# Where the second half's operands get their low parts in a Strassen-form MLP: four kept in DRAM, and the sums and low parts of a weight group on one engine

## The reference, cut to what matters

```python
hn = rmsnorm(h, norm2_g[l])
ff = jnp.square(jax.nn.relu(jnp.einsum('bsd,df->bsf', hn, w_mlp_in[l])))
h = h + jnp.einsum('bsf,fd->bsd', ff, w_mlp_out[l])
```

## Time and profile before

| | before |
|---|---|
| median of three runs | 2073.66 us (2071.78 to 2073.93) |
| the profiled execution's own time | 2072.65 us |
| its span, first to last instruction | 2070.9 us |
| PE busy | 2033.8 us (98%) |
| DVE / ACT / POOL busy | 1374.6 / 932.5 / 756.7 us |
| mean granted TensorE clock | 0.995 of full |

### The profile page before, as it was taken

The page is one execution under the profiler, slowest core; times in us unless marked ns, Lnnn a source line. Parts: engine busy times, 40 slices in busy tenths (PEclk is TensorE's granted clock), DMA queues, the critical chain, the costliest instruction groups (busy, mean ns, idle before and its releaser), DMA issues. The chain is left out here.

```text
span 2070.9 us, 26149 instructions
## 1 busy us (share of the span) xinstructions
PE 2033.8 (98%) x9474; PEld 1678.6 (81%) x9474; DVE 1374.6 (66%) x1925; ACT 932.5 (45%) x1325; POOL 756.7 (37%) x786
## 2 busy tenths in 40 slices
PE   8999999999999999999998899999999999999998
PEld 7787888888888878888886688888788888888887
DVE  3899968787778972765568655556665546555475
ACT  4456663364244561455555444544333323333253
POOL 5544465234225442644446444444120202202031
PEclk9999999999999999999999899999999999999999
DMA  6884457455555545444442233333968566565675
GB/s 219 282 276 153 143 204 274 163 167 188 194 195 193 181 165 198 143 138 144 141 142 98 87 122 128 122 132 143 365 220 303 183 225 234 189 225 179 209 238 180
DMA packets 173537, 387.32 MB, mean 187 GB/s; under 512 B 15232, under 2 KB 64480, under 8 KB 173408
## 3 DMA queue, kind: packets, MB, share of 16 engines
q1 hardware_dynamic: 153536, 313.28, 44.6%
q10 hardware_dynamic: 19872, 72.36, 10.0%
HBM read 297.51 MB, written 88.08 MB: 186 GB/s over the span
## 5 line engine op out<-in xcount | busy, mean ns | idle before, releaser
L1938 DVE TENSOR_TENSOR down_lo<-down_raw,down_hi 128x1536 fp32r<-128x1536 f32 x112 | 201.6, 1800 | 232.1 <-ACT down_hi L1452 232.1
L82 PE MATMUL acc<-down_hi 128*128 128x512 f32 x896 | 348.5, 389 | 0.0
L83 PE MATMUL acc<-down_lo,down_hi 128*128 128x512 f32 x896 | 348.5, 389 | 0.0
L84 PE MATMUL acc<-down_hi,down_lo 128*128 128x512 f32 x896 | 348.5, 389 | 0.0
L1452 ACT ACTIVATE down_hi<-down_raw 128x1536 fp32r<-128x1536 f32 x112 | 166.8, 1489 | 359.5 <-PE acc L84 193.6
L1729 DVE SCALAR_TENSOR_TENSOR acc<-u_sb,cw_col,acc 128x512 f32<-128x512 f32 x464 | 313.3, 750 | 0.3
L1379 ACT ACTIVATE ring_hi<-ring_sum 128x512 fp32r<-128x512 f32 x145 | 91.6, 632 | 272.3 <-DVE ring_sum L1840 272.3
L82 PE MATMUL acc<-xT_hi,wt 128*128 128x512 f32 x512 | 204.6, 400 | 0.2 <-DVE u_sb L2012 0.2
L84 PE MATMUL acc<-xT_hi,wt 128*128 128x512 f32 x512 | 199.8, 390 | 0.0
L83 PE MATMUL acc<-xT_lo,wt 128*128 128x512 f32 x512 | 199.4, 389 | 0.0
L82 PEld LDWEIGHTS acc<-down_hi 128*128 128x128 f32 x896 | 168.2, 188 | 35.0
(11 more groups left out here) (290 smaller groups left out, 4460.1 us busy)
## 6 DMA issues: line engine op xcount, KB each, us to landing
wt<-w_kept SPq DMA_DIRECT2D x168, 512.0 KB, 3.3
down_raw<-f_kept ACTq DMA_DIRECT2D x109, 512.0 KB, 4.2
raw_w<-in_w_mlp_in SPq DMA_DIRECT2D x32, 1024.0 KB, 5.5
f_kept<-f_tile SPq DMA_DIRECT2D x128, 256.0 KB, 2.0
down_raw<-in_w_mlp_out SPq DMA_DIRECT2D x64, 512.0 KB, 3.7
w_kept<-wt SPq DMA_DIRECT2D x48, 512.0 KB, 5.3
down_raw<-in_w_mlp_out SPq DMA_DIRECT2D x64, 256.0 KB, 3.0
down_more<-f_kept ACTq DMA_DIRECT2D x29, 512.0 KB, 5.2
```

The lines of the kernel that those rows point to most:

```text
L82: nc.tensor.matmul(out, w_hi, x_hi, start=first, stop=False, skip_group_check=onto)
L83: nc.tensor.matmul(out, w_hi, x_lo, start=False, stop=False, skip_group_check=onto)
L84: return nc.tensor.matmul(out, w_lo, x_hi, start=False, stop=last, skip_group_check=onto)
L1938: nc.vector.tensor_tensor(down_lo[slot][:, :], down_raw[d % DOWN_RAW][:, 512:], down_hi[slot][:, :].bitcast(F32), ALU.subtract).then_inc(d ...
```

## The change

It touches the 29 Strassen groups and nothing in the mixer or in the down projection's own loop.

- **Four low parts kept.** In groups 8 to 10, ACT makes the high part of half an operand at a time in a spare tile (`pre_split`), DVE its low part in another (`pre_low`), and SP stores it in DRAM (`pre_stores`, eight stores of 512 KB). These are Strassen's operands 2, 5, 3 and 7 of the second half. At the turn ACT starts their load into place (four of 1 MB) and makes the high parts again.
- **Sums.** The sum for operand 1 (h11 + h22) is made ahead in group 11, in the two spare places. The sums for 6 and 4, and the low parts of 1, 6 and 4, stay at the turn, all on DVE and in halves of 1024 columns.
- **POOL's work moved.** `a_low` of all seven places and the three `f_sum` of a group are on DVE. POOL keeps two instructions of one column in each of groups 0 to 7.
- **Order.** DVE's slot is now: add the weights of product k + 4 (`UP_LEAD = 4`), combine product k, low part of product k + 4, one `f_sum` in slots 0 to 2, then the turn's work. The row tiles are loaded, normalised and transposed one group earlier.

```diff
+UP_LEAD = 4
+        spare_hi = over("g_row", "spare_hi", [P, 2, 512], F32R)
+        spare_lo = over("y_sb", "spare_lo", [P, 2, 512], F32R, 4 * KB)
+        mul_kept = nc.dram_tensor("mul_kept", [len(PRE_LOW), P, 4, 512], F32).ap()
...
 w1_free(w):
-                    sp.wait_ge(a_lo_g, upto(NQ * s + 1, LO_ON_POOL))
-                    sp.wait_ge(a_lo_v, upto(NQ * s + 4, LO_ON_DVE))
+                    sp.wait_ge(a_lo, NQ * s + max(UP_SINGLE) + 1)
...
 SP up_group(s):
                 for p in (3, 7, 1, 6):
                     f_store(w - 1, p)
-                    if p == 7 and 1 <= s <= HT:
-                        nat_load(s - 1)
+                    if p == 7 and s < HT:
+                        nat_load(s)
+                pre_stores(s, range(0, 3))
...
+                pre_stores(s, range(3, NQ))
...
 POOL up_group(s):
-                w = group(s)
-                a_low(NQ * s + 3)
-                late_sums(w - 1)
...
+                if s < HT:
+                    nat_rstd(s)
...
 ACT:
+            def pre_split(i):
+                m, part = PRE_LOW[i // 2], i % 2
+                act.wait_ge(hn_ok, HT)
+                act.wait_ge(tr_ok, 2 * HT)
+                if m in (3, 7):
+                    act.wait_ge(pre_ok, (1 if m == 3 else 3) + part)
+                wait(act, pre_lo, i)
+                nc.scalar.activation(spare_hi[:, :, :], mul_again_src[m][:, 2 * part:2 * part + 2, :], ACT.Copy).then_inc(pre_hi, 1)
+            def mul_again(m):
+                act.wait_ge(prod_pe, used(m))
+                if m in PRE_LOW:
+                    i = PRE_LOW.index(m)
+                    act.wait_ge(pre_st, 16 * (2 * i + 2))
+                    act.dma_start(mul_lo[m].bitcast(F32), mul_kept[i]).then_inc(mul_ld[m], 16)
+                    nc.scalar.activation(mul_hi[m], mul_again_src[m][:, :, :], ACT.Copy).then_inc(mul_hi_ok, 1)
...
 DVE:
+            def pre_low(i):
+                m, part = PRE_LOW[i // 2], i % 2
+                dve.wait_ge(pre_hi, i + 1)
+                if i == 0:
+                    dve.wait_ge(tr_pe, 2 * HT)
+                else:
+                    dve.wait_ge(pre_st, 16 * i)
+                nc.vector.tensor_tensor(spare_lo[:, :, :], mul_again_src[m][:, 2 * part:2 * part + 2, :],
+                                        spare_hi[:, :, :].bitcast(F32), ALU.subtract).then_inc(pre_lo, 1)
...
                 for s in range(NS):
                     for k in range(NQ):
+                        j = NQ * s + k + UP_LEAD
+                        if j < NQ * NS:
+                            a_add(j)
                         if k > 0:
                             combine(s, k)
-                        j = NQ * s + k + LEAD
-                        if LEAD < j < NQ * NS:
-                            a_add(j)
-                            turn(s, k)
+                        if j < NQ * NS:
                             a_low(j)
+                        if k in F_SUM_AT:
+                            f_sum(group(s) - 1, F_SUMS[F_SUM_AT.index(k)])
+                        turn(s, k)
...
             def down_pass():
                 d_low(2)
+                for p in F_SUMS:
+                    f_sum(NW - 1, p)
                 d_add_parts(LEAD)
...
 PE product(s, q):
-                pe.wait_ge(*((a_lo_g, upto(j, LO_ON_POOL)) if q in LO_ON_POOL else (a_lo_v, upto(j, LO_ON_DVE))))
+                pe.wait_ge(a_lo, j + 1)
...
+                elif s == TURN and m in PRE_LOW:
+                    pe.wait_ge(mul_hi_ok, hi_again(m))
+                    pe.wait_ge(mul_ld[m], 16)
...
+PRE_LO_AT = ((8, 4), (8, 6), (9, 1), (9, 3), (9, 6), (10, 1), (10, 4), (10, 6))
+PRE_SUM_AT = ((9, 4), (9, 5), (10, 2), (10, 3), (11, 1), (11, 3))
```

More of the change, by code:

```diff
@@ L472, in hybrid_block @@
         f_sum_ok = sem("f_sum_ok")
-        f_st = {p: sem(f"f_st{p}") for p in range(1, NQ + 1)}
+        f_st = {p: sem(f"f_st{p}") for p in (1, 3, 4, 6, 7)}
         a_sum = sem("a_sum")
         a_hi = sem("a_hi")
-        a_lo_v = sem("a_lo_v")
-        a_lo_g = sem("a_lo_g")
+        a_lo = sem("a_lo")
         prod_pe = sem("prod_pe")
@@ L484, in hybrid_block @@
         pre_ok = sem("pre_ok")
+        pre_hi = sem("pre_hi")
+        pre_lo = sem("pre_lo")
+        pre_st = sem("pre_st")
+        mul_ld = {m: sem(f"mul_ld{m}") for m in PRE_LOW}
         mul_hi_ok = sem("mul_hi_ok")
@@ L815, in nat_load, with pre_stores @@
                 sp.dma_start(nat[:, :], h_t[:, HT + t, :]).then_inc(hn_ld, 16)
+            def pre_stores(s, slots):
+                for i, at in enumerate(PRE_LO_AT):
+                    if at[0] == s and at[1] in slots:
+                        m, part = divmod(i, 2)
+                        sp.wait_ge(pre_lo, i + 1)
+                        sp.dma_start(mul_kept[m, :, 2 * part:2 * part + 2, :], spare_lo[:, :, :].bitcast(F32)).then_inc(pre_st, 16)
             def up_group(s):
@@ L1801, in add_again @@
+            def add_again(m):
+                dve.wait_ge(prod_pe, used(m))
+                src, op = (h12, ALU.add) if m == 6 else (h21, ALU.subtract)
+                for part in range(2):
+                    c = slice(2 * part, 2 * part + 2)
+                    ins = nc.vector.tensor_tensor(mul_sum[m][:, c, :], src[:, c, :], sum1_again[part][:, :, :], op)
                 ins.then_inc(mul_sum_ok, 1)
-            def pre_sum(tile, op):
-                dve.wait_ge(tr_ok, 2 * HT)
-                nc.vector.tensor_tensor(tile[:, :, :], tile[:, :, :], h22[:, :, :], op).then_inc(pre_ok, 1)
@@ new lines, in turn, with f_sum @@
+                if (s, k) in PRE_SUM_AT:
+                    pre_sum(PRE_SUM_AT.index((s, k)))
+                for m in MUL_SUM_AGAIN:
+                    if (s - TURN, k) == ADD_AGAIN_AT[m]:
+                        add_again(m)
+                for m in LOW_AGAIN_AT:
+                    if (s - TURN, k) == LOW_AGAIN_AT[m]:
+                        low_again(m)
+            def f_sum(w, p):
+                a, b, op, out = {7: (F21, F22, ALU.subtract, f_tile[:, F21, :]), 1: (F11, F22, ALU.add, f_sum1[:, :]),
+                                 6: (F12, F11, ALU.subtract, f_tile[:, F12, :])}[p]
+                dve.wait_ge(f_ok[a], w + 1)
+                dve.wait_ge(f_ok[b], w + 1)
+                if p == 1:
+                    dve.wait_ge(f_st[1], w * 16)
+                elif p == 7 and w == N_PLAIN - 1:
+                    dve.wait_ge(f_sum_ok, w * len(F_SUMS))
+                nc.vector.tensor_tensor(out, f_tile[:, a, :], f_tile[:, b, :], op).then_inc(f_sum_ok, 1)
@@ L1918, in up_pass @@
                             mul_low(7, mul_sum[7], 5)
-                        if k == 6 and 1 <= s <= HT:
-                            nat_normalise(s - 1)
+                        if k == 6 and s < HT:
+                            nat_normalise(s)
             def d_add_parts(d):
@@ L2293, in up_pass @@
                     for q in range(NQ):
-                        if q == 2 and 2 <= s <= HT + 1:
-                            nat_transpose(s - 2)
+                        if q == 2 and 1 <= s <= HT:
+                            nat_transpose(s - 1)
                         product(s, q)
@@ L2629 @@
 F_SUMS = (7, 1, 6)
+F_SUM_AT = (0, 1, 2)
 TR_BANKS = [(0, 1), (4, 5)]
```

158 lines of the change are left out of this document (66 added, 92 removed).

## The result

The change takes 2049.19 us (median of four runs, 2048.61 to 2050.61) where the kernel before takes 2073.20 in the runs beside it (2071.78 to 2073.93). The ratio is 0.9886, with a 95% interval of 0.9869 to 0.9903. So it is faster by 24.0 us, and the forecast of 2052 was 2.8 us too high. The profiled execution of the changed kernel took 2049.39 us, with a span of 2047.4.

A forecast was written before the change was run, and what follows sets the result against it. PE was busy 98% of the span, its main loss being the turn, where DVE stood behind POOL's wide instructions. 27.3 us won less 1.9, 3.2 and 0.6 is 21.6; 2073.7 less that gives 2052 us, range 2046.5 to 2060.

The forecast's parts named there:

- What is taken away: The turn's 24.3 us and two waits for POOL in the first and last group, about 1.5 each: 27.3 us gone.
- Steady load at nothing: Plain groups: DVE's work of 13.6 us in a group of 19.0 costs PE nothing.
- the seam: Passage to the down projection: three f_sum ahead of the fourth step's weights cost nothing, with 2 us as bound.
- Groups 8 to 11: DVE full in groups 9 and 10, waits 1.8 us for a store at 9.3; PE loses 1.9 us at 11.0 and 11.1.
- two restarts: Slow first matmul after a PE wait: about 0.1 us for each of six waits, 0.6 in all.
- the rival of slow stores: Stores of kept parts take 5 us and DVE waits at each: 8 in place of 1.9, so 2058; chance 0.13.
- The turn: Slots 12.3 to 13.0: DVE's queue makes PE lose 0.7 at 13.2, 0.4 at 13.3, 1.5 at 13.4, 0.6 at 14.0: 3.2 us.
- the first rival: DVE copes wholly, with shorter chains than the timetable and no PE wait: 2046; chance 0.1.
- no lower clock: No clock drop taken at the turn; a rival had twice 3.2 us there and a lower-clock stretch, 2058; chance 0.12.
- The slower rival: DVE becomes the bound in every group, with a mean slot of 2.9 us: 2089; chance 0.04.

The follow-up runs named there:

- the dummies: Changed kernel plus idle POOL instructions of 1024 columns in groups 14 to 25: reading tiles once a group 2049.33 us, seven times 2145.9; only writing, seven times, 2049.15.

## Why the prediction was right

**What is taken away: 27.3 us, right.** The turn's standing still, its lower clock and the two waits for POOL in the first and last group are all gone, and no wait for POOL is left. But the reason given was only a part of it. Moving POOL's wide instructions to DVE and nothing else gives 7.4 us. All of the change but the kept parts gives 15.4 to 15.8, and the kept parts the last 8. The sum came out right because I had taken away the whole of the turn and then costed what DVE's new queue would make anew (3.2 us); the experiment without kept parts shows that this second step, not the first, carries the kept parts' value.

**Steady load at nothing: right.** I counted 13.6 us of DVE's work in a plain group of 19.0. A plain group of the changed kernel has 13.8:

```profile
1170.00:1189.00 19.00, 19.00 (x86) 15.73 (x85) 13.80 (x21) 9.81 (x16) 0.00 (x0) 1.00 0.36 125
```

No PE wait stands in the plain groups after the turn up to the end, nor at the seam, where the low part of step 3 is in time with the three f_sum ahead of it. With a lead of three the plain groups have no wait either; what the longer lead covers is in groups 10 and 13, where 2.6 us come back without it.

**Groups 8 to 11: 1.9 us and two restarts (2.1), measured 1.5.** The mechanism is as forecast: DVE waits at slot 9.3 for the store of 9.1, and PE at 11.0 and 11.1. The sizes were off, and one figure of the working does not fit the rest: a store that starts "some 3 us" before DVE comes to 9.3 and lands in 3.3 leaves a wait of 0.3, not 1.8. The 1.8 needs a lead of 1.5 us, and that is what the trace has: the store starts at 1059.60, right behind the start of the f_sum's store, and DVE is free at 1061.20. DVE's wait, and the transfers from 860 to 1440 us, the answer to the earlier trace rows:

```profile
1062.55 1.22 DVE L1819 TENSOR_TENSOR spare_lo<-h,spare_hi 128x1024 fp32r<-128x1024 f32 x1 [1.35 <-DMA mul_kept<-spare_lo]
```

```profile
nat<-h_dram SPq DMA_DIRECT2D x8, 512.0 KB, 3.4
mul_kept<-spare_lo SPq DMA_DIRECT2D x8, 512.0 KB, 2.9
hT_lo<-mul_kept ACTq DMA_DIRECT2D x2, 1024.0 KB, 5.3
```

The store lands in 2.9 us, not 3.3, and the wait is 1.35 instead of 1.8. The straight line between the store of 256 KB and the load of 1 MB (3.1), from which I had gone up, was nearer. The page of before also had 48 stores of 512 KB from another stage, with a median of 5.3 us (`w_kept<-wt`, at 33 to 342 us), which spoke for the rival of slow stores and which I had not weighed. The fit in the Trainium skill, "DMA: Bandwidth & Descriptors", section "Anatomy of one DMA", is given there for transfers that GpSimd starts; used as an estimate for this store, which SP starts, it makes 3.2 us, 0.3 above the measured 2.9. The late starts at 11.0 and 11.1 are 0.97 and 0.49 us, where I had 1.4 and 0.5.

**The turn: 3.2 us and four restarts (3.6), measured 2.4.** By the distance between starts, 13.2 lost 0.1 us (forecast 0.7 and a restart), 13.3 lost 0.3 (0.4), 13.4 lost 1.5 (1.5), its slow start another 0.1 and 14.0 lost 0.4 (0.6). The term that was too large is DVE's start. I let it enter slot 12.3 at 0.9 us after the start of 12.4, because ACT would hold up slots 1 and 2. It entered at 0.27 (1116.46, with 12.4 at 1116.19), and its slots ended at 4.5, 8.0, 12.3 and 16.5 us instead of 5.2, 8.7, 13.0 and 17.2: all by the same 0.6 to 0.7. Where I had counted too much is not shown for certain, since the working gives the 0.9 as one figure. ACT's timeline has a likely place, the start of a transfer:

```profile
1111.81 0.33 ACTq L1366 DMA_DIRECT2D mul_lo<-mul_kept  x1
1111.88 0.61 ACT L1389 ACTIVATE ring_hi<-ring_sum 128x512 fp32r<-128x512 f32 x1
1112.46 1.92 ACT L1367 ACTIVATE mul_hi<-h 128x2048 fp32r<-128x2048 f32 x1
```

The start of the transfer lies beside the activation before it, so ACT loses less than the 0.34 us that I counted for each start; in slots 12.1 and 12.2 DVE waits 0.21 us for ACT in all. The loads landed in 5.3 to 6.9 us, up to 0.6 more than I had allowed, and PE waited for none. And what DVE comes to late is what I said, the low part of operand 4:

```profile
1134.66 2.35 DVE L1828 TENSOR_TENSOR xT_lo<-mul_sum,xT_hi 128x1024 fp32r<-128x1024 f32 x2
```

It ends at 1137.01, and product 13.4 starts at 1137.12.

**Sum.** Forecast 27.3 less 5.7, measured 27.3 less 3.9. From one profiled execution to the other, 2072.65 less 2049.39 are 23.3, where I had 21.6: that is 1.7 of the 2.8 us. The rest is the step to the median. I carried over that the median stands 1.0 above the profiled execution of before; of the changed kernel it stands 0.2 below. Both errors lie on the same side, so the total did not come out by one cancelling the other. (The range's lower end, 2046.5, leaves out the first rival's 2046, which the text says it takes in.)

**The rivals.** DVE did not cope wholly. The stores are fast. There is no lower clock: the longest wait is 1.19 us and the clock reads 1.00 behind it. The slower rival is excluded by 691 ns for the weights' sum: the 874 of the earlier trace rows were POOL's doing, which the dummies show from the other side. Its first half, the advice to hand work from a full VectorE to another engine (the Trainium skill, "Perfetto Trace Analysis", section "Optimizing Scalar/DVE Operations"), would have cost 7 us here with GpSimd as that engine, by the run with the three sums given back. Its own warning about the shared read port is what decides. What I had wrong in my own weighing was the size of the small instructions. The prediction charged POOL's wide ones with the turn and its small ones with two waits of 1.5 us. They also cost 6 to 7 us where DVE is full. The earlier trace rows showed them, as 874 ns where 690 are due, but no wait of PE in before did, since its groups 9 and 10 were not full.

What stays open: low parts given back to POOL without the sums were not run, so the 7 us of the sums and the 8 of both do not say what the low parts cost alone. And the parts do not add up: 7.4 for the wide instructions, 7 to 8 for the small ones and 8 for the kept parts overlap, since all stand in the same queue on DVE.

## What to carry to other kernels

When an engine stands behind another that shares a port with it, cost the change twice: once for the standing still that goes, and once for the queue that the standing hid, with the whole work put in a row slot by slot. Work moved to GpSimd to relieve VectorE is paid for by VectorE if GpSimd reads tiles and VectorE's instructions have two tiles as inputs, at more than it saved (1.1 us against 0.61 here), so it is free only where VectorE has slack. And where a full engine reuses one spare tile through a store, the store's place in its queue and the distance between the uses are part of the sum: spreading the uses won 1.3 to 1.5 us, moving the store ahead about 0.6.

## What the runs showed of the hardware

- One POOL instruction of 1024 columns with two tiles as inputs (2.39 us) makes a DVE instruction of 512 columns, also with two tiles, last 2.91 us instead of 0.69. It has no effect on a DVE instruction with a PSUM bank and one tile as inputs (678 ns). A POOL memset (958 ns) has none on the DVE instruction with two tiles (693 ns).
- The holding seems to go both ways: a sum of 512 columns on POOL was seen at 1.29 us, and lasts 1.49 to 1.75 in the mean in the versions where POOL makes it beside DVE's work. That DVE is what lengthens it is read from this difference, not from a run of its own.
- In the Strassen groups a store of 512 KB from SP lands in 2.9 us (median of eight), one of 256 KB in 2.0 to 2.1, a load of 1 MB in 5.3 to 6.9.
- A transfer's start on ACT's queue (0.33 us at 1111.81) overlaps the activation ahead of it (1110.07 to 1111.98).
